# Moving the SBUF tiles of a ten-layer fp32 network: the padding tiles taken out of the address layout

## What is computed

```python
for i in range(2):
    f = swiglu_ffn(rmsnorm(x, ffn1_norm_pre[i]), ffn1_w_in[i], ffn1_w_out[i])   # 1024 -> 2x2816 -> 1024
    x = x + 0.5 * rmsnorm(f, ffn1_norm_post[i])
    p = rmsnorm(x, mix_norm_pre[i]) @ mix_w_in[i]
    y_a = gated_deltanet(qkv, z, beta_logit, a_logit, ...)    # 8 heads, chunks of 64
    y_b = conformer_conv(glu_in, ...)                         # 31 taps per channel, layer norm
    x = x + rmsnorm((g_a * y_a + g_b * y_b) @ mix_w_out[i], mix_norm_post[i])
    ...                                                       # second swiglu_ffn, as the first
for i in range(4):
    h = (gla_mixer, mla_mixer, conv_mixer, gla_mixer)[i](x, ...)
    x = layer_norm(ALPHA * x + h, ...)
    x = layer_norm(ALPHA * x + square(relu(x @ mlp_w1[i])) @ mlp_w2[i], ...)    # 1024 -> 4096 -> 1024
    x = x + sigmoid(x @ ple_w_gate[i]) * (p[i] @ ple_w_proj[i])
```

## Time and profile before

| | |
|---|---|
| Median of 3 runs | 3016.11 us |
| The profiled execution's own time | 3015.88 us |
| Its span, first to last instruction | 3014.1 us |
| TensorE matmul busy | 2883.0 us (96%), 15292 matmuls |
| VectorE busy | 1934.4 us (64%) |
| ScalarE busy | 1537.6 us (51%) |
| Mean granted TensorE clock | 0.977 |
| HBM traffic | 466.48 MB read, 155 GB/s |

### The profile page before, as it was taken

One profiled execution on the slowest core, in us unless ns is written; L12 is line 12 of the kernel. 1 busy time (PEld: TensorE's weight loads), 2 busy tenths in 40 slices (PEclk: granted clock), 3 DMA queues, 4 the chain that ended last, 5 costly groups with the idle time before them and its releaser, 6 DMA issues.

```text
span 3014.1 us, 38314 instructions
## 1 busy us (share of the span) xinstructions
PE 2883.0 (96%) x15292; PEld 2443.9 (81%) x15292; DVE 1934.4 (64%) x2858; ACT 1537.6 (51%) x2235; POOL 73.8 (2%) x99
## 2 busy tenths in 40 slices
PE   7999998899999999988999999999999999999999
PEld 6879987678878799876788878887888878887887
DVE  5556987575565569876755676465646765567645
ACT  5544744355555447443655545555545445564554
POOL 0000000000000000000000000000000000000000
PEclk9999999899999999998999999999999999999999
DMA  7534510245555444102455525543555555453552
GB/s 280 188 134 161 175 50 22 101 168 204 189 180 189 138 161 171 54 22 92 166 210 189 177 94 208 184 175 112 200 189 181 192 185 184 158 195 109 187 183 83
DMA packets 127809, 470.03 MB, mean 156 GB/s; under 512 B 14494, under 2 KB 14654, under 8 KB 126480
## 3 DMA queue, kind: packets, MB, share of 16 engines
q1 hardware_dynamic: 124560, 453.08, 43.0%
q0 software_dynamic: 3072, 14.51, 1.4%
HBM read 466.48 MB, written 1.05 MB: 155 GB/s over the span
## 4 chain that ended last, share of the span: by engine, by line
PE 80%; DVE 12%; ACT 5%; issue 2%; POOL 1%; DMA 0%; SPq 0%; POOLq 0%; ACTq 0%; DVEq 0%
PE ps L590 77%; DVE w_lo_part L1966 2%; DVE hc L2273 2%; PE ps L767 2%; DVE conv_acc L2198 1%; ACT w_hi_part L1421 1%; PE ps L627 1%; DVE wx_lo_part L1966 0%; DVE h_lo_part L2009 0%; ACT wx_hi_part L1421 0%; DVE x_res L2110 0%; DVE zs L2416 0%; ACT gdn_rhs L1696 0%; POOL gdn_gate L2762 0%; DVE x_res L2168 0%
## 5 line engine op out<-in xcount | busy, mean ns | idle before, releaser
L1966 DVE TENSOR_TENSOR w_lo_part<-w_raw,w_hi_part 128x1024 fp32r<-128x1024 f32 x459 | 552.8, 1216 | 346.9 <-ACT w_hi_part L1421 344.5
L1421 ACT ACTIVATE w_hi_part<-w_raw 128x1024 fp32r<-128x1024 f32 x459 | 477.5, 1054 | 402.4 <-PE ps L590 402.1
L590 PE MATMUL ps<-w_hi_part,h_hi_part 128*128 128x512 f32 (+1 forms) x1348 | 542.3, 402 | 32.6 <-DVE w_lo_part L1963 8.3
L590 PE MATMUL ps<-w_hi_part,h_lo_part 128*128 128x512 f32 (+1 forms) x1348 | 528.6, 392 | 0.0
L590 PE MATMUL ps<-w_lo_part,h_hi_part 128*128 128x512 f32 (+1 forms) x1348 | 528.0, 392 | 0.0
L1966 DVE TENSOR_TENSOR wx_lo_part<-wx_raw,wx_hi_part 128x1024 fp32r<-128x1024 f32 x222 | 268.2, 1219 | 203.2 <-ACT wx_hi_part L1421 201.2
L1421 ACT ACTIVATE wx_hi_part<-wx_raw 128x1024 fp32r<-128x1024 f32 x222 | 231.6, 1055 | 226.5 <-PE ps L590 226.4
L590 PEld LDWEIGHTS ps<-w_hi_part,h_hi_part 128*128 128x128 f32 x1348 | 258.3, 192 | 91.5 <-issue 18.9
L590 PEld LDWEIGHTS ps<-w_hi_part,h_lo_part 128*128 128x128 f32 x1348 | 257.7, 191 | 54.7
L590 PEld LDWEIGHTS ps<-w_lo_part,h_hi_part 128*128 128x128 f32 x1348 | 258.9, 192 | 48.5
L590 PE MATMUL ps<-wx_hi_part,h_hi_part 128*128 128x512 f32 x684 | 271.4, 397 | 6.9 <-ACT lv L1759 2.2
(11 more groups left out here) (437 smaller groups left out, 4899.1 us busy)
## 6 DMA issues: line engine op xcount, KB each, us to landing
w_raw<-in_weights SPq DMA_DIRECT2D x569, 512.0 KB, 3.3
wx_raw<-in_weights SPq DMA_DIRECT2D x288, 512.0 KB, 3.3
row<-in_rows POOLq DMA_DIRECT2D x8, 1024.0 KB, 4.9
row<-in_rows POOLq DMA_DIRECT2D x8, 512.0 KB, 4.0
const<-in_const SPq DMA_DIRECT2D x1, 1088.0 KB, 16.0
x_res<-in_x SPq DMA_DIRECT2D x2, 512.0 KB, 6.8
ple_p<-in_p POOLq DMA_DIRECT2D x4, 256.0 KB, 4.7
out<-x_res SPq DMA_DIRECT2D x2, 512.0 KB, 2.6
```

The lines of the kernel that those rows point to most:

```text
L590: return nc.tensor.matmul(out, lhsT, rhs_, start=start, stop=stop, skip_group_check=True)
L1421: A(hi_of(s)[:, 0:wd], raw_of(s)[:, 0:wd], ACT.Copy).then_inc(*up("w_hi", u))
L1966: V.tensor_tensor(lo_of(s)[:, 0:wd], raw_of(s)[:, 0:wd], hi[:, 0:wd], ALU.subtract).then_inc(*up("w_lo", u))
```

## The change

The padding tiles are removed (only `glu_end` stays, with 256 floats where it had 384), `conv_ln` shrinks from 32 to 8 floats and stands behind `gdn_norm`, and `mla_norm` gets room of its own behind `rope` where it lay under the scores' tile `msc1`. `W_BASE` and `W_TOP`, which only size the unused tile `below`, change with it. No line that issues an instruction is touched.

```diff
-W_BASE, W_TOP = 129024, 228864
+W_BASE, W_TOP = 128512, 229344
...
-        sb("first_gap", [P, 96])
         w_raw = sb("w_raw", [P, NS_IN, UW])
...
         cols = sb("cols", [P, COLS.n])
-        sb("cols_gap", [P, 56])
         row = sb("row", [P, 2, 2, D])
         neghalf = sb("neghalf", [P, 16])
         st = sb("stats", [P, 4, 32])
-        sb("stats_gap", [P, 112])
...
         gate = sb("gdn_gate", [P, 12, 40], F32, m1)
-        lnm = sb("conv_ln", [P, 32], F32, m1)
         gnw = sb("gdn_norm", [P, 1, GDK], F32, m1)
+        lnm = sb("conv_ln", [P, 8], F32, m1)
         mw = ExitStack()
         glu = sb("glu", [P, KC, CONVB - 1 + SEQ], F32, mw)
-        sb("glu_gap", [P, 16], F32, mw)
         state = sb("gdn_state", [P, GH, GDK], F32, mw)
...
-        sb("glu_end", [P, 384], F32, m1)
+        sb("glu_end", [P, 256], F32, m1)
...
         mkr = sb("mkr", [P, SEQ], F32, mw3)
-        mnorm = sb("mla_norm", [P, 1, 512], F32, mw3)
         mw3.close()
...
         rope = sb("rope", [P, SEQ], F32, m3)
+        mnorm = sb("mla_norm", [P, 1, 512], F32, m3)
...
         cpad = sb("cpad", [P, KC, 2 + SEQ], F32, m4)
-        sb("cpad_gap", [P, 112], F32, m4)
         cz = sb("cz", [P, KC, SEQ], F32, m4)
```

## The result

The changed kernel takes 3036.11 us (median of 4 runs, 3034.19 to 3037.81) against 3016.24 us for the kernel before (4 runs, 3015.88 to 3017.45). The ratio is 1.0065, with a 95% interval of 1.0047 to 1.0083: slower by 20 us, clear of the 0.2% that can be told from nothing. The profiled execution has a span of 3032.2 us, 18.1 more than in the earlier trace rows.

What follows compares the result with a forecast made beforehand. The prediction took TensorE's matmul cadence to bound the kernel. Its terms for TensorE, VectorE, ScalarE and DMA were each 0, summing to 0 us against the profiled 3015.88 us: forecast 3016 us, range 3008 to 3047 us.

Steps and rivals of the forecast that it cites:

- What bounds the kernel: Whole kernel: TensorE, busy 2883.0 of 3014.1 us and 80% of the chain; its cadence of 226.9 ns per matmul sets the time.
- What the change is: All engines and queues: only addresses alter, no instruction, semaphore or order of work; 0 removed and 0 added.
- The TensorE term: Matmuls reading tiles at new addresses: 0 ns more each, taken from the 64 `gdn_gate` matmuls.
- The upper bound: TensorE's other bound, from `mla_masked` 32 B above a multiple of 64: 33 and 21 ns more than aligned matmuls.
- The first rival: TensorE pays for starts off a boundary: 2 ns on all 15292 matmuls, 31 us slower, 3047 us; chance 0.20.
- VectorE, ScalarE: Their accesses at new addresses: 0 taken, at most 1.9%, which is 7 us for VectorE and 3 us for ScalarE.
- DMA: Weight transfers and the start: dearer packets stay hidden behind SyncE's waits; 0 taken, 1 us if the start takes a tenth more.
- The freer rival: Engines reading side by side disturb each other less: 5 us on VectorE and ScalarE, the same 1% in mixers' matmuls, 3006 us; chance 0.11.

## Why the prediction was wrong, point by point

- **What bounds the kernel** held in what matters: TensorE's pace sets the time, and the whole 20 us came from it. But "that cadence, times the number of matmuls" is not the kernel: 226.9 ns holds for streams of 512 columns, and times all 15292 it would be 3470 us, more than the span. The kernel is a sum over forms, and the forecast was not worked out from that product.
- **What the change is** held: no instruction, no order and no wait changed, and the new addresses were as worked out. But the paragraph noted that the distances among `w_raw`, `w_hi_part`, `w_lo_part` and `h_hi_part` stayed as they were, and did not ask about the other distances. `hid` had gone from 0 to 96 above `w` and 32 above `wx` by 256, and `wx` from 0 to 64 above `h`. That was the change.
- **The TensorE term, taken as 0, is the step that failed.** It came from the 64 `gdn_gate` matmuls, which began 32 B above a multiple of 64 and took 275 ns, and take 275 after the change, at a multiple of 64 (154240). But they load a broadcast column or stream 8 columns, and tell nothing of a stream of 512 columns beside a load of 128. The other look, that `w_hi_part` and `wx_hi_part` both take 390 ns, was read as "where a tile lies does not matter"; both were at a distance of 0 from `hid`. In place of 0 the term measured 17.5 us of busy time for the `hid` forms and some 4 for `wx`, and it hangs on the distance between the tile that streams and the tile that is loaded, which the prediction did not consider. Its last sentence, that an aligned stream of 512 columns may have an advantage no row could show, saw the gap in the rows but looked for it in alignment.
- **The upper bound** from `mla_masked` was no bound of this at all: at a multiple of 512 it takes the same 321 and 426 ns.
- **The first rival** had the place (TensorE, 512 column streams), the sign, and 31 us for 20. Its mechanism was wrong: with all starts 32 B off there is no cost, with `hid` back on a multiple of 512 there is. Its 2 ns were spread over all 15292 matmuls, where 2592 pay 6.8 ns each. That the range, 3008 to 3047 us, holds the measured 3036 is owed to this rival, and so to luck. Its threshold, a cadence over 227.3 ns, is what the chain shows: 22.17 us for 96 are 230.9.
- **VectorE, ScalarE** at 0: right, 476 to 477 ns for the earlier trace rows before and after, ScalarE busy for 1538.0 us against 1537.6, and the run that moved only the feed-forward's other tiles changed nothing.
- **DMA** at 0: right in its effect, with landings of 3.3 us or 3.4 and SyncE waiting as before. Whether a packet pays its extra beats was not needed and stays open.
- **The freer rival** put its gain into engines disturbing each other, and that was not found. A gain from an uneven distance does exist, but within TensorE and for 256 column streams: 4 us by the means of the runs, 6 by the medians, once it is taken alone.

The Trainium skill says of such a case, in "SBUF — State Buffer", section "Who interferes with whom", that TensorE's read for the moving operand and its read for the weights are independent, and that only the port pair that VectorE and GpSimd share causes contention. These runs speak against the first: moving the two `hid` parts by 32 B, with every other tile at its old remainder by 512, lengthens the matmuls that load them from 390 to 396 ns, and moving everything else of the stage in their stead does not. So the cost of a matmul hangs on both addresses, which two independent reads would not lead one to expect. The measurement decides.

**What stays open.** That the stream of one matmul and the load for the next get in each other's way in the memory fits all runs, but is argued, not shown; no row gives the two reads apart. Nor is it shown why `wx_lo_part` is spared past `hid` and `wx_hi_part` is not where the loaded tile lies 64 B lower. With it 32 or 96 B lower there are few matmuls, but they pay: in two of the runs above `conv_hi_part` lay so below `wx` (32 in the changed kernel with its stage tiles back, 96 in the one with all large distances at a multiple of 512), and its 24 matmuls past `wx_lo_part` took 395 ns in each, where they take 390 in the kernel before. Why 256 column streams gain, and whether distances under 32 B matter, is open too.

## What to carry to other kernels

When nothing but addresses changes, compare a matmul's mean by form before anything else: the tile that TensorE streams and the tile that it loads as weights meanwhile should be a multiple of 256 B apart where streams have 512 columns. Here, for fp32r and loads of 128 x 128, that alone was worth 0.6%, or 1.3% for all weights. Absolute alignment was worth nothing, so a layout needs a few padding bytes between the groups, not round addresses. A row that shows "address does not matter" only counts for the pattern it has: ask what it holds constant.

## What the runs showed of the hardware

- With a distance that is a multiple of 256 B between what streams and what is loaded, matmuls of 512 fp32r columns follow each other at 226.9 ns; with the loaded tile 32, 64, 96 or 128 B higher by 256, `hid` forms are recorded 5 to 8 ns longer, with it 64 B lower 0 to 5.
- Matmuls of 256 columns go the other way: 287 to 283 ns with the loaded tile 32 B higher, 287 to 284 with it 32 B lower, 284 to 281 with it 64 B higher.
- Reads of VectorE at any multiple of 4 B cost the same, 470 to 482 ns for 256 columns over all 480 taps after the change.
